# A hand-written slot schedule in a fused two-layer decoder kernel: the delta-rule mixers start a round earlier and run stretched

## The reference

```python
q = (xt @ w_q).reshape(n_tok, 8, 2, 128)                 # 8 heads, 2 halves
scores = einsum('thcd,ckd->thck', q, sub_keys)           # 128 keys a half
top_s, top_i = top_k(scores, 16)                         # then the best 16 of 16 x 16 sums
expert_id, gate = ...                                    # 128 experts a token
act = gelu(einsum('td,tkd->tk', xb, u_tab[eb]))          # a dot with each expert's u row
out = einsum('tk,tkd->td', gate * act, v_tab[eb])        # a sum of the experts' v rows
```

## Time and profile before

| | |
|---|---|
| median of three runs | 3198.05 us (3196.58 to 3205.08) |
| the profiled execution: its own time | 3192.53 us |
| its span, first to last instruction | 3190.8 us |
| TensorE matmul / weight load, busy | 78% / 44% of the span |
| VectorE, ScalarE, GpSimd, busy | 77%, 32%, 37% |
| DMA | 1185.06 MB in 2 queues, mean 371 GB/s |

### The profile page before, as it was taken

The page is one execution under the profiler, slowest core; times in us unless marked ns, Lnnn a source line. Parts: engine busy times, 40 slices in busy tenths (PEclk is TensorE's granted clock), DMA queues, the critical chain, the costliest instruction groups (busy, mean ns, idle before and its releaser), DMA issues.

```text
span 3190.8 us, 35616 instructions
## 1 busy us (share of the span) xinstructions
PE 2497.1 (78%) x11944; PEld 1402.8 (44%) x11944; DVE 2465.9 (77%) x7332; ACT 1012.2 (32%) x1878; POOL 1174.9 (37%) x1041
## 2 busy tenths in 40 slices
PE   7889998777677888898877899989786776665565
PEld 6776554343233454555533466556442332221111
DVE  8646889877778788878777767887977777878874
ACT  3522433221112545653211344565321211121111
POOL 0002444434444343424344433333435343434441
PEclk8889999897878999999988999999998878887777
DMA  5227999999999999979999989998999999999995
GB/s 210 67 108 288 409 406 400 406 373 419 419 418 385 419 404 379 381 293 398 416 418 415 390 334 382 382 382 325 417 417 420 417 419 419 420 414 414 416 416 244
DMA packets 182393, 1185.06 MB, mean 371 GB/s; under 512 B 19649, under 2 KB 25793, under 8 KB 50881
## 3 DMA queue, kind: packets, MB, share of 16 engines
q0 software_dynamic: 147456, 1073.81, 82.8%
q1 hardware_dynamic: 34752, 108.98, 8.9%
HBM read 1180.61 MB, written 2.10 MB: 371 GB/s over the span
## 4 chain that ended last, share of the span: by engine, by line
PE 37%; DMA 30%; DVE 16%; ACT 7%; issue 6%; POOL 4%; DVEq 0%; ACTq 0%; SPq 0%; POOLq 0%
DMA arena<-uv_tab,cols 29%; PE ps L737 13%; PE xps L670 8%; DVE arena L2134 5%; POOL arena L627 4%; PE ps L670 3%; DVE scr L2145 2%; ACT L1376 1%; PE xps L1079 1%; PE xps L1130 1%; PE ps L709 1%; PE xps L1153 1%; DVE arena L2229 1%; PE xps L1150 1%; DVE cols L2037 1%
## 5 line engine op out<-in xcount | busy, mean ns | idle before, releaser
L627 POOL DMA_INDIRECT arena<-uv_tab,cols x1024 | 1170.7, 1143 | 1960.9 <-PE ps L737 1291.7
L737 PE MATMUL ps<-arena,scr 128*64 128x512 f32 x4096 | 1194.4, 712 | 512.3 <-DVE scr L2145 511.8
L2134 DVE CUSTOM_DVE_ANT_0 arena<-arena 128x1024 f32<-128x1024 f32 x1024 | 1250.7, 1222 | 344.8 <-DMA arena<-uv_tab,cols 303.0
L737 PEld LDWEIGHTS ps<-arena,scr 128*64 128x64 f32 x4096 | 280.4, 153 | 1131.6 <-DVE scr L2145 711.0
L1376 ACT ACTIVATE cols<-cols 128x2 f32<-128x2 f32 x512 | 104.1, 203 | 1441.3 <-DVE cols L2134 1439.7
L2145 DVE SCALAR_TENSOR_TENSOR scr<-sel,cols 128x64 f32<-128x64 f32 x1024 | 243.4, 279 | 196.2 <-ACT cols L1376 190.7
L670 PE MATMUL xps<-arena,wring 128*128 128x256 f32 x1600 | 384.0, 388 | 11.8 <-DVE arena L2290 4.2
L670 PEld LDWEIGHTS xps<-arena,wring 128*128 128x128 f32 x1600 | 296.7, 193 | 89.4 <-issue 36.4
L670 PE MATMUL ps<-arena,wring 128*128 128x256 f32 x1184 | 281.2, 392 | 4.6 <-DVE arena L1747 4.1
L670 PEld LDWEIGHTS ps<-arena,wring 128*128 128x128 f32 x1184 | 226.4, 196 | 80.6 <-issue 45.4
L1376 ACT ACT_TABLE_LOAD x161 | 206.6, 1283 | 2.9
(11 more groups left out here) (438 smaller groups left out, 2788.5 us busy)
## 6 DMA issues: line engine op xcount, KB each, us to landing
wring<-wall SPq DMA_DIRECT2D x176, 512.0 KB, 7.9
arena<-uv_tab,cols POOLq DMA_INDIRECT x1024, 12.6
arena<-wall SPq DMA_DIRECT2D x16, 512.0 KB, 9.5
h<-xT SPq DMA_DIRECT2D x2, 1024.0 KB, 11.5
arena<-glu_w SPq DMA_DIRECT2D x2, 1024.0 KB, 13.1
out<-arena SPq DMA_DIRECT2D x4, 512.0 KB, 17.3
arena<-s_b SPq DMA_DIRECT2D x1, 512.0 KB, 9.5
arena<-s_bt SPq DMA_DIRECT2D x1, 512.0 KB, 10.3
```

What stands on the lines that cost most here:

```text
L627: pool.indirect_dma_start(out=whole_row(at), out_offset=None, in_=uv_tab, in_offset=bass.IndirectOffsetOnAxis(ap=ids[g % 2][:, k:k + 1], a ...
L737: mm = pe.matmul(ps[4 + half][64 * j:64 * j + 64, :], wdiag[:, b % PAIRS, j, :], pair_row(at + j, 1)[:, T * half:T * half + T], start=(g % ...
L2134: dve.tensor_tensor_reduce(u, u, xrep[:, k % 2, :], 1.0, 0.0, ALU.mult, ALU.add, dots[g % 2][:, k:k + 1]).then_inc(s["dot_done"], 1)
```

## The change

Each group of generators gets a map from its old slot to a new one, `at + (t - raw) * by`. Layer 0's second mixer keeps its start and is stretched by 1.05. The delta-rule mixer of the first half starts at slot 256 in place of 272 and is stretched by 1.08, that of the second half at 512 in place of 528, stretched by 1.11. The eight output chunks stand 2.5, 2 and 2 slots apart (before stretching) in place of 1.5. The queries of group 1 start in round 11 in place of 10. The mask building, its two index patterns on GpSimd and the decay rate move from round 15 to 14.

```diff
-    r = (-2, 10, 30, 46)[gi] + q
+    r = (-2, 11, 30, 46)[gi] + q
...
+def spread(part):
+
+    raw, at, by = SPREAD[part]
+    return lambda t: at + (t - raw) * by
+
+
+SPREAD = {"even": (1, 1, 1.05), 0: (16 * 17, 16 * 16, 1.08), 1: (16 * 33, 16 * 32, 1.11)}
...
 def out_step(gi):
 
-    return 1.5
+    return (0, 2.5, 2, 2)[gi]
+
+
+def out_slot(gi):
+
+    return spread(("even", 0, 1)[gi - 1])
+
+
+def g_slot(g):
+
+    return spread("even") if g else None
...
-                todo.append((out_at(gi) + out_step(gi) * c, 1, "o_mm", 8 * (gi - 1) + c, (20, 76)[gi // 2] + c))
+                todo.append((out_slot(gi)(out_at(gi) + out_step(gi) * c), 1, "o_mm", 8 * (gi - 1) + c, (20, 76)[gi // 2] + c))
...
-                todo.append((front_at(m, p) + front_step(p) * i, 1, "m_mm", (4 * m + p) * 6 + i,
+                todo.append((spread(m)(front_at(m, p) + front_step(p) * i), 1, "m_mm", (4 * m + p) * 6 + i,
...
-    def __init__(self, start, steps):
-        self.start, self.steps, self.due = start, steps, start
+    def __init__(self, start, steps, slot=None):
+        self.start, self.steps, self.slot = start, steps, slot or (lambda t: t)
+        self.due = self.slot(start)
 
     def upto(self, now):
 
         while self.due <= now:
             step = next(self.steps, None)
-            self.due = math.inf if step is None else self.start + step
+            self.due = math.inf if step is None else self.slot(self.start + step)
...
-                if r == 15:
+                if r == 14:
...
-            paced += [Paced(first_at(m), gates_in(m)) for m in range(2)]
-            paced += [Paced(z_at(m, 0), z_in(m)) for m in range(2)]
+            paced += [Paced(first_at(m), gates_in(m), spread(m)) for m in range(2)]
+            paced += [Paced(z_at(m, 0), z_in(m), spread(m)) for m in range(2)]
...
-            paced += [Paced(15 * TOPK + 2, masks())]
+            paced += [Paced(14 * TOPK + 2, masks())]
```

More of the change, by code:

```diff
@@ L194, in weight_order @@
             at = x[1] if x[0] == "u" else (8, 4, 12, 16)[x[1]] + x[0]
[L195 removed]
+            todo.append((spread("even")(proj_at(g, x)) if g else proj_at(g, x), 1, "e_mm", PROJ_N[g, x], at))
     for gi in range(4):
@@ L1231, in out_rows @@
                 mm.then_inc(s["hsum"], 1)
[L1233 removed]
+            paced = [Paced(proj_at(g, ("u", 0)), u_rows(g), g_slot(g)) for g in range(2)]
             paced += [Paced(-147.5, pair_weights()), Paced(-104, second_norm())]
[L1235 to L1238, removed]
[L1239 to L1243 removed]
+            paced += [Paced(state_at(g, 0) - 2.5, states(g), g_slot(g)) for g in range(2)]
+            paced += [Paced(head_in_at(g, hd), head_in(g, hd), g_slot(g)) for g in range(2) for hd in range(HG)]
+            paced += [Paced(head_at(g, hd), head(g, hd), g_slot(g)) for g in range(2) for hd in range(HG)]
+            paced += [Paced(-80, first_glu()), Paced(mixed_at(1) + 1, glu(1), g_slot(1))]
+            paced += [Paced(first_at(m), gates_in(m), spread(m)) for m in range(2)]
+            paced += [Paced(z_at(m, 0), z_in(m), spread(m)) for m in range(2)]
+            paced += [Paced(back_at(m, p), back(m, p), spread(m)) for m in range(2) for p in range(4)]
+            paced += [Paced(front_at(m, p), front(m, p), spread(m)) for m in range(2) for p in range(4)]
+            paced += [Paced(out_at(gi), out_rows(gi), out_slot(gi)) for gi in range(1, 4)]
             for x in range(-360, 0):
@@ L1663, in out_rows @@
                 act.activation(nrt, nrt, ACT.Exp, scale=-0.5).then_inc(s["h_root"], 1)
-            paced = [Paced(proj_at(g, ("u", 0)), u_rows(g)) for g in range(2)]
+            paced = [Paced(proj_at(g, ("u", 0)), u_rows(g), g_slot(g)) for g in range(2)]
             paced += [Paced(-147, pair_weights()), Paced(-112, second_norm())]
[L1667 to L1674, removed]
+            paced += [Paced(head_in_at(g, hd), head_in(g, hd), g_slot(g)) for g in range(2) for hd in range(HG)]
+            paced += [Paced(head_at(g, hd), head(g, hd), g_slot(g)) for g in range(2) for hd in range(HG)]
+            paced += [Paced(-81.5, first_glu()), Paced(mixed_at(1), glu(1), g_slot(1))]
+            paced += [Paced(first_at(m), gates_in(m), spread(m)) for m in range(2)]
+            paced += [Paced(z_at(m, 0), z_in(m), spread(m)) for m in range(2)]
+            paced += [Paced(back_at(m, p), back(m, p), spread(m)) for m in range(2) for p in range(4)]
+            paced += [Paced(front_at(m, p), front(m, p), spread(m)) for m in range(2) for p in range(4)]
+            paced += [Paced(out_at(gi), out_rows(gi), out_slot(gi)) for gi in range(1, 4)]
             for x in range(-360, 0):
@@ L1712, in _ @@
                         to_rows(*rows[now - 0.5])
-                    if r == 15 and k == 2:
+                    if r == 14 and k == 2:
                         decay_rate()
@@ L2320, in out_rows @@
                 mm.then_inc(s["xn_ready"], 1)
-            paced = [Paced(state_at(g, 0), states(g)) for g in range(2)]
-            paced += [Paced(head_at(g, hd), head(g, hd)) for g in range(2) for hd in range(HG)]
-            paced += [Paced(mixed_at(g), glu(g)) for g in range(2)]
-            paced += [Paced(15 * TOPK + 2, masks())]
+            paced = [Paced(state_at(g, 0), states(g), g_slot(g)) for g in range(2)]
+            paced += [Paced(head_at(g, hd), head(g, hd), g_slot(g)) for g in range(2) for hd in range(HG)]
+            paced += [Paced(mixed_at(g), glu(g), g_slot(g)) for g in range(2)]
+            paced += [Paced(14 * TOPK + 2, masks())]
             paced += [Paced(TOPK * (PH * t + 8), tile_done(t)) for t in (1, 3, 4, 5, 6)]
[L2327 to L2331, removed]
+            paced += [Paced(first_at(m), gates_in(m), spread(m)) for m in range(2)]
+            paced += [Paced(z_at(m, 0), z_in(m), spread(m)) for m in range(1)]
+            paced += [Paced(back_at(m, p), back(m, p), spread(m)) for m in range(2) for p in range(4)]
+            paced += [Paced(front_at(m, p), front(m, p), spread(m)) for m in range(2) for p in range(4)]
+            paced += [Paced(out_at(gi), out_rows(gi), out_slot(gi)) for gi in range(1, 4)]
             for x in range(-360, 0):
```

## The result

The changed kernel takes 3226.69 us (3223.93 to 3229.3) against 3199.19 us before: 1.0077 of the time, 95% interval 1.006 to 1.0093. I had forecast 3187 us, 0.35% faster, in a range up to 3204. It is slower, not faster, and stands 23 us above the upper end of the range.

What follows compares the result with a forecast made beforehand. The prediction took the gathers as the floor, with time lost where TensorE's peaks make them pause. Terms -6.6 - 2.2 - 4.4 + 0.9 + 1 sum to -11.3 us, taking the median from 3198 to 3187 us, range 3168 to 3204.

Steps and rivals of the forecast that it cites:

- The bound: Whole kernel: gathers are the floor at about 419 GB/s; time is lost where they pause, in mixer stretches behind TensorE's peaks.
- The ring rival: Eight ring places absorb a round's excess under 10 us; 14 us more gained, 3173 us; chance 0.2.
- my 0.8: Rounds 30 to 45: share of the excess taken as lost time, applied to the new order; 1.0 in rounds 16 to 29.
- the excess: Per round, TensorE's counted work over the DMA's demand (gathers plus weight chunks), where positive; 50.8 us in rounds 16 to 29.
- Second mixer of layer 0, -6.6 and -2.2: Later output chunks cut round 8's excess from 8.8 to 2.2 us, -6.6; rounds 1 to 7 from 7.6 to 5.4, -2.2.
- First mixer, -4.4: First delta-rule mixer, rounds 16 to 29: excess 50.8 becomes 46.4 us, times 1.0, giving -4.4 us.
- Waits inside the mixer, taken as cancelling: More room between mixer pieces saves 0 to 18 us; starting at a tile's end with a full ring costs 0 to 10.
- Second mixer, +0.9: Second delta-rule mixer, rounds 30 to 45: peak moves from round 34 to 33; excess 82.7 becomes 83.8, times 0.8: +0.9 us.
- Gather of slot 736, +1 of 0 to +7: This gather waits for the later last norm of `xn`, leaving about 6.6 us later, mostly covered by DMA work: +1 us.
- The sign that I had named: Slot 736's gather issued 3 dots later without a dot wait over 2 us would show the forecast right.
- The slower rival: Mixers start in a drained stretch at a tile's end, rounds 32 to 34 taking 170 us; 3206 us in all, chance 0.12.
- The signs named beforehand: Right if rounds 8, 24, 34 take about 48, 52, 44 us; wrong if round 8 stays 55 or 32 to 34 exceed 165.

Runs made afterwards that it cites:

- e12: Kernel before with layer 0's output chunks 2.5 slots apart and the second delta-rule mixer's eight z chunks moved: 0.9939, 3175.49 us against 3196.47.
- the control: Run e9: changed source with all its numbers set back to the old ones, so the instruction order of the kernel before: 1.0001 of its time.
- e7: Kernel before with only the output chunks after layer 0's second mixer 2.5 slots apart in place of 1.5: 0.9992.
- e1: Kernel before with layer 0's part alone: second mixer stretched by 1.05, output chunks 2.5 slots apart, group 1's queries from round 11: 1.0058.
- e13: Kernel before with only the first delta-rule mixer stretched by 1.035 from its old start, slot 272; output chunks 1.5 apart: 1.0057.
- e4: Kernel before with only the first delta-rule mixer started at slot 256, unstretched, and masks in round 14; output chunks 1.5 apart: 1.0011.
- e8: Kernel before with only the second delta-rule mixer started at slot 512 and stretched by 1.11; output chunks 1.5 slots apart: 0.9994.
- e16: Kernel before with first delta-rule mixer at slot 256, stretched 1.08 by piece starts only, inner steps old; masks in 14, output chunks 1.5 apart: 1.0076.

## Why the prediction was wrong

- *The bound.* That the gathers are the floor and that TensorE's peak in round 34 costs time was right: e12 took the peak down and won 18 us in three rounds. (Round 24 loses more, 20.7 us against 17.4 in the control, but lowering its peak gave nothing.) The ring rival was nearer there than my 0.8: at a count of 57 us over a demand near 50, round 34 runs at 407 GB/s and loses 1.6 us, where 0.8 of the excess is 5.6. (Its time of 3173 holds only one of its two terms: 0.8 of 83.8 less 52.9 is the 14 us, and half of the first mixer's 46.4 would be 23 more.)
- *Second mixer of layer 0, -6.6 and -2.2.* The first is borne out by e7's trace (19.7 to 13.0 us of loss). The step that failed is that the stretch and the queries cost nothing besides: each costs 0.3% when timed alone, and the stretch +8.6 us in its trace, in rounds 7 and 8. Together with the step they make the part 0.58% slower (e1). I had counted only TensorE's work by rounds.
- *First mixer, -4.4.* Measured +11 us alone. The failed step is "The losses in the two mixer stretches are 1.0 and 0.8 of it", the excess, and "That is the scale for the new order". The scale held for one arrangement only. TensorE's count in round 24 fell as said and the round still took 57.9 us at 230 GB/s. I read the match of 50.8 and 50 us as a cause. In the new round 24 it is ScalarE's share of the chain that doubled, from 12.0 to 22.1 us, while TensorE's halved. A count of one engine's work doesn't see that. Which meeting of pieces makes it is open.
- *Waits inside the mixer, taken as cancelling.* I let "others get 8 to 11% more room" stand against a full ring. e13 shows that room is no gift: 3.5% of it costs 18 us. By how much each single wait grew is open.
- *Second mixer, +0.9.* Right in kind: round 33 took 64.5 us with TensorE at 61.78, and alone with the old step the mixer is 0.9994.
- *Gather of slot 736, +1 of 0 to +7.* Mis-sized: round 45 loses 5 us by it. The norm came late, as its place says, and GpSimd stood for 12.21 us until then. The last gather before it had left at 2434.54, and the dots at 2447.80 and 2450.51 found their rows without a wait, so I had been wrong to put slot 735's landing next to its dot: the DMA had run dry. The sign that I had named, no dot wait over 2 us, held at 1.91 and missed the loss: the pause shows in the DMA's rate, not in a dot's wait. The Trainium skill's fit (DMA: Bandwidth & Descriptors, Anatomy of one DMA), by which I had estimated 4.4 us and no cost, is too short here: 6.2 us passed from this gather's issue to its dot's start, with 1.91 us of that waiting for the rows.
- *The slower rival* named the drained start behind a tile. e4 puts that at 0.11% for the first mixer, within its interval of nothing, and e8, which starts the second at 512, is 0.9994. Its own sign, round 33 under 300 GB/s, did not come either (338). It had the direction and not the mechanism.
- *The signs named beforehand.* Round 8 was to take 48 us at over 400 GB/s; it took 53.1 at 318. Round 24 was to take 52; it took 57.9. Rounds 32 to 34 took 163.9 us, just under the 165 that I had set as the sign of failure, and round 34 took 53.0 in place of 44. Rounds 16 to 29 took 684.6 us in place of 660, rounds 30 to 45 776.2 in place of 767.

## What to carry to other kernels

When four in-order engines share one schedule, count what each order makes them wait for, not only how full the fullest is: round 24 went from 55.3 to 47.2 us of TensorE and lost 5 us more. Read the chain of a round as well as its busy times. Move the few pieces that make a measured peak, a few at a time, and leave the rest at their place; eight z chunks and eight output chunks gave 0.6% where a smooth stretch of everything lost 0.8%. Check every global wait, such as a ring that grows at one slot, against each end that the new timetable makes later.

## What was not expected of the hardware

Executions differ by up to 8 us of loss in rounds where the order of instructions is the same (46 to 63: 36.9 in the control, 42.7 in e4, 35.0 in e13), and by up to 5 in rounds 1 to 15 (18.0 in e13, 19.7 in the control, 23.0 in e8). So a trace shows where time goes, but terms under some 5 us need the timed runs too, or a place, like round 45, that loses nothing in any other trace.

In rounds 46 to 63 the scatter goes by when a kernel ran. In e1 to e8 round 48 loses 3.1 to 7.9 us and round 56 5.1 to 9.0, whatever the change; in e9 to e16 it is 0.6 at most and 1.8 to 3.3. The kernel before moved with them: its medians are 3201 and 3204 us beside e1 to e8, 3194 to 3196 beside the later ones. What differed in the chip is not shown. Only ratios to runs of the same time are safe.
